# Heads' squares as three bf16 parts in blocks 2 and 3 too, and a block 2 that adds its second row earlier

## The reference

```python
def rmsnorm(x, g):
    x32 = x.astype(jnp.float32)
    y = x32 * lax.rsqrt(jnp.mean(x32 * x32, axis=-1, keepdims=True) + EPS)
    return (y * g.astype(jnp.float32)).astype(x.dtype)
...
h = rmsnorm(x, norm_g)
proj = h @ w_in                       # 1024 -> 2576 columns: q, k, v, low rank, gates, pool, mem
gk = jax.nn.log_sigmoid(gk_lr @ w_gk_up + b_gk) / 16
o_gla = gla_chunked(q, k, v, gk)      # 4 heads, chunks of 64, a state handed from chunk to chunk
o_gla = rmsnorm(o_gla, gla_norm_g)    # over the 128 values of each head: "the head's mean square"
o_gla = o_gla * silu(gate_g)
o_pool = (multiscale_pool(u_p) @ pool_w) * pool_scale * silu(gate_p)
o_mem = memory_attention(q_m, mem_n, w_mem_kv) * silu(gate_m)
x = x + concat([o_gla, o_pool, o_mem]) @ w_out
y = rmsnorm(x, final_g)
```

## Time and profile before

| | us |
|---|---|
| median of 3 runs | 1352.45 (1351.65 to 1354.74) |
| the profiled execution | 1352.88 |
| its span in the trace | 1351.1 |
| PE busy | 1328.5 (98%) |
| DVE busy | 921.9 (68%) |
| ACT busy | 817.1 (60%) |
| POOL busy | 450.7 (33%) |

### The profile page before, as it was taken

The page is one execution under the profiler, slowest core; times in us unless marked ns, Lnnn a source line. Parts: engine busy times, 40 slices in busy tenths (PEclk is TensorE's granted clock), DMA queues, the critical chain, the costliest instruction groups (busy, mean ns, idle before and its releaser), DMA issues.

```text
span 1351.1 us, 35800 instructions
## 1 busy us (share of the span) xinstructions
PE 1328.5 (98%) x14667; PEld 1003.7 (74%) x14667; DVE 921.9 (68%) x1664; ACT 817.1 (60%) x1481; POOL 450.7 (33%) x353
## 2 busy tenths in 40 slices
PE   6999999999999999999999999999999999999998
PEld 5788668577695877859687695968769596886954
DVE  6886667575656757666676857667685766758556
ACT  7886645655647466565655656566574756657353
POOL 2111164136522335243353432335343233534100
PEclk9999999999999999999999999999999999999999
DMA  9575656664673847747595877768596675858631
GB/s 386 190 209 200 243 187 216 209 227 192 216 256 115 330 155 240 260 125 300 186 305 173 280 256 212 263 186 307 183 280 246 211 267 185 311 188 280 251 92 49
DMA packets 155997, 302.92 MB, mean 224 GB/s; under 512 B 76112, under 2 KB 93776, under 8 KB 152656
## 3 DMA queue, kind: packets, MB, share of 16 engines
q1 hardware_dynamic: 155136, 299.75, 65.4%
q10 hardware_dynamic: 720, 1.06, 0.2%
HBM read 249.39 MB, written 34.60 MB: 210 GB/s over the span
## 4 chain that ended last, share of the span: by engine, by line
PE 87%; DVE 5%; ACT 4%; issue 2%; DMA 2%; SPq 0%; ACTq 0%; DVEq 0%
PE bank L863 28%; PE bank L822 21%; PE bank L936 11%; PE bank L842 10%; PE bank L1088 2%; PE bank L1114 2%; PE bank L1108 2%; DVE arena L1955 2%; PE bank L1179 1%; PE bank L1211 1%; ACT arena L1423 1%; PE bank L1099 1%; PE bank L877 1%; PE bank L1131 1%; PE bank L1072 1%
## 5 line engine op out<-in xcount | busy, mean ns | idle before, releaser
L863 PE MATMUL bank<-arena,ring 128*128 128x128 f16 x4032 | 239.0, 219 | 0.5
L863 PE MATMUL bank<-arena,wres 128*128 128x128 f16 x4032 | 237.0, 219 | 0.6 <-DVE arena L1966 0.5
L863 PEld LDWEIGHTS bank<-arena,ring 128*128 128x128 f16 x4032 | 228.9, 98 | 5.5 <-DVE arena L1856 2.4
L863 PEld LDWEIGHTS bank<-arena,wres 128*128 128x128 f16 x4032 | 227.7, 98 | 3.2 <-issue 2.1
L822 PE MATMUL bank<-wv,arena 128*128 128x512 f16 x768 | 168.7, 379 | 0.2 <-DVE wv L1842 0.2
L2457 POOL TENSOR_TENSOR arena<-arena 128x1024 f16<-128x1024 f32 x32 | 70.1, 2212 | 235.8 <-ACT arena L1287 192.7
L822 PE MATMUL bank<-ring,arena 128*128 128x512 f16 x672 | 148.7, 379 | 0.0
L2449 POOL TENSOR_TENSOR arena<-arena 128x1024 f32<-128x1024 f32 (+2 forms) x42 | 64.9, 1545 | 231.9 <-ACT arena L1269 229.7
L822 PEld LDWEIGHTS bank<-wv,arena 128*128 128x128 f16 x768 | 75.0, 98 | 87.6 <-DVE wv L1842 0.4
L936 PE MATMUL bank<-ring,arena 128*128 128x512 f16 x576 | 129.6, 379 | 0.3
L822 PEld LDWEIGHTS bank<-ring,arena 128*128 128x128 f16 x672 | 64.8, 98 | 77.2 <-issue 3.0
(11 more groups left out here) (293 smaller groups left out, 2372.1 us busy)
## 6 DMA issues: line engine op xcount, KB each, us to landing
ring<-out_parts SPq DMA_DIRECT2D x104, 512.0 KB, 4.9
ring<-gate_parts SPq DMA_DIRECT2D x92, 512.0 KB, 7.7
ring<-side_parts SPq DMA_DIRECT2D x92, 512.0 KB, 6.9
ring<-out_sums SPq DMA_DIRECT2D x64, 512.0 KB, 5.0
arena<-in_xt SPq DMA_DIRECT2D x16, 1024.0 KB, 6.1
arena<-in_x SPq DMA_DIRECT2D x32, 512.0 KB, 5.2
out<-arena SPq DMA_DIRECT2D x31, 512.0 KB, 3.0
arena<-in_w_out SPq DMA_DIRECT2D x24, 512.0 KB, 4.7
```

What stands on the lines that cost most here:

```text
L863: mm = nc.tensor.matmul(ap, w[:, p, k, j * P:(j + 1) * P], x_part(r, b)[:, k, :], start=fresh and j == 0 and k == 0 and n == 0, stop=k == ...
```

## The change

`splits_heads` is a new condition, true from block 2 (`WHOLE - 2`) to 14, where the condition was true from block 4. It decides who cuts the squares into three parts, on PE, ACT and DVE. `head_parts(i)` counts what earlier blocks have added to the two semaphores `sq_round` and `sq_rest`: 4 for each of blocks 2 and 3, 6 for each later block. The other edits replace the old counts by it. Separately, block 2 now calls `rows(3)` ahead of `pool_gate`, as blocks 3 to 6 do.

```diff
+        def splits_heads(i, last):
+            return not last and (not isinstance(i, int) or i >= WHOLE - 2)
+
+        def head_parts(i):
+
+            if isinstance(i, int) and i < WHOLE:
+                return 4 * (i - WHOLE + 2)
+            return 6 * i - 6 * WHOLE + 10
...
                 def head_ms(p):
-                    if is_whole(i) or last:
+                    if not splits_heads(i, last):
                         pe.wait_ge(o_sq, 2 * i + p + 1)
                         nc.tensor.matmul(bank[6 + p][:, :], ones[:, :], osq[p], start=True,
                                          stop=True).then_inc(pe_msq, 1)
                         return
-                    pe.wait_ge(sq_round, 6 * (i - WHOLE) + p + 5)
-                    pe.wait_ge(sq_rest, 6 * (i - WHOLE) + p + 5)
+                    pe.wait_ge(sq_round, head_parts(i) + p + 3)
+                    pe.wait_ge(sq_rest, head_parts(i) + p + 3)
...
                     if first:
                         act.wait_ge(cp[GG if p == 0 else PM], 4)
                         silu(p, GG if p == 0 else PM)
-                    elif not is_whole(i) and not last:
+                    elif splits_heads(i, last):
                         for turned in d_turn:
                             act.wait_ge(turned, 32 * (i + 1))
                         nc.scalar.activation(o_part[p][0], bank[b][:, :].rearrange("p (a t) -> p a t", a=2),
                                              ACT.Square).then_inc(sq_round, 1)
                 if first:
                     nc.scalar.preload_act_table_set(EXP_LN)
-                elif not is_whole(i) and not last:
+                elif splits_heads(i, last):
                     for p in range(NPAIR):
-                        act.wait_ge(sq_rest, 6 * (i - WHOLE) + p + 3)
+                        act.wait_ge(sq_rest, head_parts(i) + p + 1)
                         nc.scalar.activation(o_part[p][1], osq[p], ACT.Copy).then_inc(sq_round, 1)
...
                 def osq_rest_of(p):
                     dve.wait_ge(o_sq, 2 * i + p + 1)
-                    dve.wait_ge(sq_round, 6 * (i - WHOLE) + p + 3)
+                    dve.wait_ge(sq_round, head_parts(i) + p + 1)
                     nc.vector.tensor_tensor(osq[p], osq[p], o_part[p][0], ALU.subtract).then_inc(sq_rest, 1)
...
-                if not is_whole(i) and not last:
+                if splits_heads(i, last):
                     osq_rest_of(0)
                     osq_rest_of(1)
                     osq_lo_of(0)
                     osq_lo_of(1)
...
-                if makes_sums(i):
+                if makes_sums(i) or makes_gates(i):
                     rows(3)
                 if not is_seven(i, last):
                     pool_gate()
...
-                elif not makes_sums(i):
+                elif not makes_sums(i) and not makes_gates(i):
                     rows(3)
```

More of the change, by code:

```diff
@@ L757, in rms_parts @@
             def rms_parts(n):
-                pe.wait_ge(sq_round, 6 * (n - WHOLE) - 4)
-                pe.wait_ge(sq_rest, 6 * (n - WHOLE) - 4)
+                pe.wait_ge(sq_round, head_parts(n - 1))
+                pe.wait_ge(sq_rest, head_parts(n - 1))
                 for k in range(3):
@@ L1601, in step @@
                     if not last:
-                        act.wait_ge(sq_rest, 6 * (i - WHOLE) + 1)
+                        act.wait_ge(sq_rest, head_parts(i) - 1)
                         nc.scalar.activation(x_sum[1], sq[:, 0, :], ACT.Copy).then_inc(sq_round, 1)
@@ L2150, in step @@
                     if not last:
-                        dve.wait_ge(sq_round, 6 * (i - WHOLE) + 1)
+                        dve.wait_ge(sq_round, head_parts(i) - 1)
                         nc.vector.tensor_tensor(sq[:, 0, :], sq[:, 0, :], x_sum[0], ALU.subtract).then_inc(sq_rest, 1)
@@ L2154, in step @@
                     if not last:
-                        dve.wait_ge(sq_round, 6 * (i - WHOLE) + 2)
+                        dve.wait_ge(sq_round, head_parts(i))
                         nc.vector.tensor_tensor(x_sum[2], sq[:, 0, :], x_sum[1], ALU.subtract).then_inc(sq_rest, 1)
@@ L2327, in osq_rest_of @@
                     dve.wait_ge(o_sq, 2 * i + p + 1)
-                    dve.wait_ge(sq_round, 6 * (i - WHOLE) + p + 3)
+                    dve.wait_ge(sq_round, head_parts(i) + p + 1)
                     nc.vector.tensor_tensor(osq[p], osq[p], o_part[p][0], ALU.subtract).then_inc(sq_rest, 1)
                 def osq_lo_of(p):
-                    dve.wait_ge(sq_round, 6 * (i - WHOLE) + p + 5)
+                    dve.wait_ge(sq_round, head_parts(i) + p + 3)
                     nc.vector.tensor_tensor(o_part[p][2], osq[p], o_part[p][1], ALU.subtract).then_inc(sq_rest, 1)
-                if not is_whole(i) and not last:
+                if splits_heads(i, last):
                     osq_rest_of(0)
```

## The result

The changed kernel takes 1354.51 us (median of 22 runs), the kernel before beside it 1352.49 us: a ratio of 1.0016, 95% interval 1.0009 to 1.0022, or 1.2 to 3.0 us slower. Forecast were 1353.8 us, 1.3 us slower. The profiled execution took 1354.54 us, its span 1352.8 us against 1351.1. One run of the kernel before (6119.14 us), and one beside e5 to e8 (2791.18 us), are far outside the rest and stand outside the ratios.

What follows compares the result with a forecast made beforehand. PE, busy 98% of the span, was taken to bound the kernel. Block 2 +1.55 us and block 3 -0.25 us gave +1.3 us, 1353.8 us on the median; the range given was 1351.4 to 1355.8 us.

Steps and rivals of the forecast that it cites:

- PE's own work: Ends of blocks 2 and 3: six bf16 products take 1.38 us, not 1.81; 0.43 us less per block without waits.
- Block 2, step by step: End of block 2: DVE's subtractions stand behind POOL's instructions, PE waits, and the block costs 1.53 us, taken as 1.55.
- second rest: Block 2's second DVE subtraction: ready at 270.77 inside a POOL instruction, ends at 273.02, 0.55 us behind it.
- first low part: Block 2: DVE subtraction standing behind POOL's next instruction, ending at 275.79, just in time for 276.10.
- second low part: Block 2's last DVE subtraction: stands behind POOL's third instruction, ends at 278.56; PE waits until 278.6 instead of 276.8.
- first rest: Block 2's first DVE subtraction: ready at 269.10, ends at 269.78, ahead of POOL's first addition at 270.12.
- the rival of one more turn: Block 2: first subtraction also stands behind POOL, projection 4.3 us late, run 1356.5 us; chance 0.09.
- The rival of milder locks: Block 2: each subtraction takes 1.56 us, PE waits nowhere, -0.43 us in each block, run 1351.6 us; chance 0.12.
- The move: Block 2's second half row ahead of the pool's product: worth some 2.7 us with the splits, nothing alone.
- Block 3: End of block 3: residual at 362.31, logits between 369.37 and 369.73, gain 0.07 to 0.43 us, taken as 0.25.
- The sum: Whole run: block 2 +1.55 and block 3 -0.25 give +1.3 us, 1353.8 us on the median.
- the late residual: Block 3's residual arrives late as in block 4, a loss of 0.70 us there, run 1354.7 us; chance 0.19.

Runs made afterwards that it cites:

- e5: Kernel before with only block 2's second half row moved ahead of the pool's and memory's products, no new split: 1352.49 us, ratio 1.0001.
- e8: Changed kernel with POOL's combination waiting for block 2's last subtraction and the residual's second half ahead of the sums' write: 1350.94 us, ratio 0.9989.
- e4: Changed kernel with POOL's combination of the queries' weights waiting for block 2's last subtraction: 1352.55 us, ratio 1.0001 to the kernel before.
- e6: Changed kernel with each of POOL's four additions of the queries' weights cut into two halves: 1352.46 us, ratio 1.0001 to the kernel before.
- e3: Changed kernel with block 2's second half row left behind the pool's and memory's products: 1359.56 us, ratio 1.0052 to the kernel before.
- e9: Changed kernel run twice more, unedited, for further traces: 1354.44 and 1354.38 us.
- e7: Changed kernel with the residual's second half asked for ahead of the output weights' sums' write in blocks 3 to 6: 1352.96 us, ratio 1.0005.
- e2: Block 2 alone splits, its second half row moved ahead of the pool's product; block 3 as in the kernel before: 1354.08 us, ratio 1.0010.
- e1: Block 3 alone splits its heads' squares; block 2 as in the kernel before, its half row not moved: 1351.89 us, ratio 0.9997.

## Why the prediction was right

**PE's own work.** Six products took 1.39 us in block 3 (forecast 1.38), and with POOL out of the way both blocks are shorter by 0.43 and 0.42 us (e4).

**Block 2, step by step.** With the trace's offset of 0.32 us taken off, forecast and trace are: second rest ends 273.02 and 273.02; first low part ends 275.79 and 275.78; second low part ends 278.56 and 278.54; half rows end 279.89 and 279.87; projection starts 279.99 and 280.01. The last agreement is partly luck. The forecast had PE wait 0.1 us for the half row there, and the trace has no such wait: PE took up its products at 278.69, not 278.6, and 0.74 us for three of them and 0.55 for the low-rank products bring it to 279.98 by its own work. The block cost 1.51 to 1.55 us. The first rest was ahead of POOL, as forecast, so the rival of one more turn did not happen; it was ready 1.1 us before POOL's first addition. The rival of milder locks, 1.56 us for each subtraction, is refuted by the changed kernel's own 2.25, 2.84 and 2.83 us, and sharing in place of standing by e6. Here the Trainium skill's rule of an exclusive lock (SBUF — State Buffer, "SBUF: two separate sides") agrees with the three ends at 0.54 to 0.55 us, at either length of POOL's instructions.

**The move.** "Worth some 2.7 us": the wait was 2.72 us (e3). Its whole worth is 5.05, because of the clock, which the forecast did not have.

**Block 3.** The residual arrived at 364.11, less 1.86 is 362.25 (forecast 362.31). The logits came at 371.39, less 1.86 is 369.53 (forecast 369.37 to 369.73). The gain is 0.27 us (taken: 0.25). The residual landed 6.36 us after its issue before and after, so the subtractions did not make it late. In e9's traces the logits come 5.93 and 6.07 us behind the low-rank products, so the gain lies between 0.27 and 0.41 us.

**What was off.** The sum was 1.3 us and the median moved by 2.0. The steps give 1.55 - 0.27 = 1.28 in the trace; 0.7 us is not in them. The interval, 1.2 to 3.0 us, just holds the 1.3, so some of the 0.7 may be no more than scatter. I had weighed the late residual for block 3 only, with "its waits occur once" as an argument that it is rare. In truth it comes in nearly every trace without e7's edit, behind one of blocks 4 to 6 (behind two in e6), at 1.0 to 1.5 us; only e2's has none. The table's "late" without block 4's own part, which the 0.27 already has, averages 1.54 us over the three traces of the changed kernel (1.34, 1.41, 1.86) and 1.18 over the two whose heads are as before (before and e5: 1.26, 1.10). That would be 0.36 us of the missing 0.7, but kernels that differ in nothing at these blocks scatter by more than that, so it is not a shown effect of the splits. The place is less a matter of chance: in all six traces without e7's edit in which blocks 2 and 3 both split, a long one (1.04 to 1.49 us) stands behind block 6, in before, e1 and e5 behind block 4 or 5 and never behind 6. Why was not found: without e7's edit the residual landed 6.0 to 8.1 us after its issue, with it 3.7 to 5.4, and a long issue did not make it later. A fall of the clock in a few runs may add to the mean, and little to the median.

## What to carry to other kernels

Before work is moved to VectorE beside a busy GpSimd, count turns, not durations: here each operation with both inputs in SBUF (the on-chip memory) that met a GpSimd instruction stood until its end, and four subtractions that take 3.8 us from first start to last end (e4) took 9.5 beside a queue of long ones. Hold GpSimd back by a semaphore where its results are not due, or cut its instructions shorter; either took the loss in that block back here, though against the kernel before neither whole run is measurably faster. And a wait seen once in a trace is not rare when its cause stands at several places.

## What the runs showed that I had not expected

- PE's granted clock fell to 0.50 (1.2 GHz) behind a wait of 1.78 us in e2's trace, and not in four other traces with the same wait (the changed kernel three times, and e7). The 72 products behind it took 9.69 us in place of 8.02.
- Behind a wait of 1.77 us and 1.4 us of work it fell in e3, during a second wait of 2.72 us, and stayed at 0.50 for some 6 us; the fall cost 2.19 us, nearly as much as the second wait. All five timed runs of e3 show the lower mean clock (0.997 or 0.998).
- An issue of the residual's transfer on SP behind blocks 3, 5 and 6 took 0.66 us, and behind block 4 from 0.95 to 1.68 us in the traces without e7's edit. A long one did not go with a late arrival: in e4, behind block 4, it was issued at 437.31 for 1.66 us and landed 6.1 us later.
